# Hybrid decoder trunk: where in the projection's order the state space outputs, the attention weighing and the recurrent gates stand

## The reference, cut to what matters

```python
for l in range(2):
    h = x * (1 + scale) + shift                      # scale, shift, gate from cond @ w_ada[l]
    proj = h @ w_in[l]                               # 2048 -> 6144, twelve chunks of 512
    pa, pb, pc, pd = split(proj)
    y_a = a_b * causal_conv3(a_c * a_x) * silu(a_g)
    y_b = dilated_attention(q, k, v) * silu(b_g)     # 8 heads of 64, three dilation patterns, relative bias
    xc  = causal_conv4(c_x) + bias                   # recurrent branch
    r, i = sigmoid(xc @ wa + ba), sigmoid(xc @ wx + bx)      # 8 blocks of 64 x 64: the gates
    y_c = scan(a(r), sqrt(1 - a*a) * i * xc) * silu(c_g)
    bu  = d_u @ B                                    # complex, 16 channels -> 64 states, 32 groups: the drives
    s   = complex_scan(lambda, bu)
    y_d = glu(gelu(Re(C @ s) + D * d_u)) * silu(d_g) # Re(C @ s): the state space outputs
    x = layer_norm(ALPHA * x + (1 + gate) * (concat(y_a, y_b, y_c, y_d) @ w_out[l]))
```

## Time and profile before

| | |
|---|---|
| median of three runs | 1719.42 us (1717.12 to 1720.55) |
| the profiled execution | 1719.88 us |
| its span | 1718.1 us |
| PE matmul busy | 1653.5 us (96%) |
| DVE busy | 1164.0 us (68%) |
| ACT busy | 754.4 us (44%) |
| POOL busy | 179.4 us (10%) |
| mean granted clock of PE | 0.982 |
| DMA | 373.58 MB, 217 GB/s over the span |

### The profile page before, as it was taken

One profiled execution on the slowest core, in us unless ns is written; L12 is line 12 of the kernel. 1 busy time (PEld: TensorE's weight loads), 2 busy tenths in 40 slices (PEclk: granted clock), 3 DMA queues, 4 the chain that ended last, 5 costly groups with the idle time before them and its releaser, 6 DMA issues.

```text
span 1718.1 us, 22890 instructions
## 1 busy us (share of the span) xinstructions
PE 1653.5 (96%) x7696; PEld 1269.4 (74%) x7696; DVE 1164.0 (68%) x2325; ACT 754.4 (44%) x988; POOL 179.4 (10%) x245
## 2 busy tenths in 40 slices
PE   5889999999999999999999999999999999999996
PEld 0347778778777877878887777777877777777885
DVE  1438975995697589657867685588378458743758
ACT  1316535554553555421127454654555465432112
POOL 2001111111111111000001111111111111100000
PEclk9799999999999999999999999999999999999998
DMA  9998899999999998978748888888988888775524
GB/s 364 339 317 212 204 245 245 219 220 221 242 226 231 238 220 204 215 248 274 246 145 203 196 206 195 205 199 208 209 203 208 192 200 204 188 184 218 196 94 116
DMA packets 317297, 373.58 MB, mean 217 GB/s; under 512 B 30584, under 2 KB 227536, under 8 KB 314512
## 3 DMA queue, kind: packets, MB, share of 16 engines
q1 hardware_dynamic: 288608, 270.57, 49.4%
q0 software_dynamic: 27936, 101.72, 33.1%
q10 hardware_dynamic: 656, 0.17, 0.0%
HBM read 263.89 MB, written 10.99 MB: 160 GB/s over the span
## 4 chain that ended last, share of the span: by engine, by line
PE 74%; DVE 17%; DMA 5%; issue 3%; ACT 1%; DVEq 0%; SPq 0%; ACTq 0%
PE bank L1232 19%; PE bank L1187 15%; PE bank L1197 15%; PE bank L1188 14%; DVE work L1562 6%; DMA pro<-in_w_ada 4%; PE bank L1219 2%; DVE work L1421 1%; DVE work L1422 1%; DVE y_t L1570 1%; PE bank L915 1%; DVE carry L1570 1%; DVE ada_acc L1570 1%; PE bank L1127 1%; PE bank L966 1%
## 5 line engine op out<-in xcount | busy, mean ns | idle before, releaser
L1187 PE MATMUL bank<-op,w_hi 128*128 128x512 f32 x1456 | 581.5, 399 | 0.2 <-ACT w_hi L671 0.2
L1188 PE MATMUL bank<-op,w_hi 128*128 128x512 f32 x1456 | 569.1, 391 | 0.0
L671 ACT ACTIVATE w_hi<-raw 128x1024 fp32r<-128x1024 f32 x188 | 199.2, 1059 | 418.9 <-PE bank L1188 286.5
L1197 PE MATMUL bank<-op,w_lo 128*128 128x512 f32 x1456 | 361.9, 391 | 3.6 <-DMA w_lo<-raw 3.6
L1187 PEld LDWEIGHTS bank<-op,w_hi 128*128 128x128 f32 x1456 | 274.1, 188 | 77.7 <-issue 21.6
L1197 PEld LDWEIGHTS bank<-op,w_lo 128*128 128x128 f32 x1456 | 273.7, 188 | 62.7 <-DMA w_lo<-raw 6.0
L1188 PEld LDWEIGHTS bank<-op,w_hi 128*128 128x128 f32 x1456 | 274.3, 188 | 56.6 <-issue 1.9
L604 POOL DMA_DIRECT2D w_lo<-raw x190 | 165.3, 870 | 1333.3 <-ACT w_lo L674 1124.3
L674 ACT ACTIVATE w_lo<-raw 128x1024 fp32r<-128x1024 f32 x188 | 198.4, 1055 | 98.1 <-PE bank L1197 96.6
L1232 PE MATMUL bank<-w_hi,op 128*128 128x512 f32 x960 | 232.2, 392 | 2.1 <-ACT op L861 2.1
L1232 PEld LDWEIGHTS bank<-w_hi,op 128*128 128x128 f32 x960 | 181.0, 189 | 41.0 <-issue 3.2
(11 more groups left out here) (228 smaller groups left out, 1521.1 us busy)
## 6 DMA issues: line engine op xcount, KB each, us to landing
raw<-in_w_in SPq DMA_DIRECT2D x192, 512.0 KB, 4.6
w_lo<-raw POOLq DMA_DIRECT2D x190, 512.0 KB, 5.3
ada_in<-in_w_ada SPq DMA_DIRECT2D x256, 256.0 KB, 4.6
pro<-in_w_ada SPq DMA_DIRECT2D x32, 1024.0 KB, 10.1
raw<-in_w_out SPq DMA_DIRECT2D x64, 512.0 KB, 4.7
y_t<-in_x SPq DMA_DIRECT2D x2, 2048.0 KB, 12.9
bias_t<-bias_rows_scratch SPq DMA_DIRECT2D x16, 256.0 KB, 5.7
y_t<-in_x SPq DMA_DIRECT2D x4, 1024.0 KB, 8.1
```

The lines of the kernel that those rows point to most:

```text
L671: act.activation(w_hi[:, n % NHL, :], raw[:, n % NRAW, :], ACT.Copy).then_inc(s.hi_done.sem, 1)
L1187: pe.matmul(o, w_hi[:, n % NHL, w], op_hi[k], start=k == 0, stop=False)
L1188: mm = pe.matmul(o, w_hi[:, n % NHL, w], op_lo[k], start=False, stop=False)
L1197: mm = pe.matmul(o, w_lo[:, m % NHL, w], op_hi[k], start=False, stop=k == KT - 1)
```

## The change

Three placements in PE's order are changed, and nothing else. The gates' `put` now stands behind those of the drives, and its gap is 5 in place of 6 (in layer 0's step 0 the gap stays the same, 7). `s5_outputs` goes from gap 19 to gap 20. `weigh` 0 goes from gap 18 to 20 and `p_turn` 1 from 18 to 20; `weigh` 1 goes from 20 to 21 and `p_turn` 2 from 20 to 21; `p_turn` 0 (16) and `weigh` 2 (22) stay. So gap 20 now holds `s5_outputs`, `weigh` 0, `p_turn` 1; gap 21 `weigh` 1, `p_turn` 2; gaps 6, 18 and 19 are empty. The programs of ACT, DVE, SP and POOL are the same as before.

```diff
                     first = l == 0 and begun
                     put(EARLY if first else 3, s5_turn)
-                    put(EARLY + 3 if first else 6, lru_gates)
                     for q, at in enumerate((EARLY + 2 if first else 5, EARLY + 2 if first else 5, 12, 12)):
                         put(at, s5_drive, q)
-                    put(19, s5_outputs)
+                    put(EARLY + 3 if first else 5, lru_gates)
+                    put(20, s5_outputs)
                     for t, at in enumerate((9, 10, 12, 13)):
                         put(at, scores, t)
                     put(10, v_turn)
-                    for g, (at_turn, at_weigh) in enumerate(((16, 18), (18, 20), (20, 22))):
+                    for g, (at_turn, at_weigh) in enumerate(((16, 20), (20, 21), (21, 22))):
                         put(at_weigh, weigh, g)
                         put(at_turn, p_turn, g)
                     put(HALF - 1, ada_sum)
```

## The result

| | before | after |
|---|---|---|
| median | 1719.29 us (1717.12 to 1720.97, 6 runs) | 1754.0 us (1746.8 to 1758.48, 6 runs) |
| profiled execution, its span | 1719.88, 1718.1 us | 1753.59, 1751.8 us |
| mean granted clock | 0.982 | 0.980 |

The ratio is 1.0197, 95% interval 1.0177 to 1.0218: slower by 34 us, where I had forecast slower by 4.

The account below looks back on a forecast made before the run. PE, 96% busy, was taken to bound the kernel, so waits and change-overs removed were set against late low weights: -4.7 - 1.9 + 6.0 + 4.8 = +4.2, a median of about 1723.6 us, 80% range 1713.5 to 1730.

Parts of the forecast that it names:

- Part A: Outputs in layer 0's steps 1 to 3: their wait for DVE goes, 1.56 a time, three times, -4.7 us.
- Part B: Merged outputs, weighing and turning: fewer PE change-overs, 0.24 a step over eight steps, -1.9 us (0 to -3.3).
- Part C, the gates behind the drives: Gap 5 on PE: an exit of 0.13 us saved in each of seven steps.
- Part C, the issue of tile 9's add DMA: ACT's table load begins 0.90 later, so tile 9's add DMA goes out at 311.08 in place of 310.18.
- Part C, its landing: Tile 9's add DMA lands in 6.1 us, costing 0.85 a step, seven times: +6.0.
- upper half of the range: Tile 9's landing cost, range -0.9 to +31 (+1.7 to +12 for 5.5 to 7.0): larger costs likelier by the DMA page.
- Part D: End of a step: tile 22's low weights just due, tile 23's late in seven steps, +4.8 us (0 to +12).
- What would show it: Signs: no outputs' wait; tile 9 waits 0.5 to 1; L1197 DMA waits 15 or more; ACT waits 7 at n = 21.
- The second rival: Tile 9 not late, its add DMA landing in 5.0 or less: about -7, 1712.4 us; chance 0.18.
- the first: Rival: only tile 9 late, add DMAs of tiles 22 and 23 landing within 5.5: +0.4, 1719.8 us; chance 0.32.
- The third, bunching: Rival: landings of 7.0 at tiles 9 and 23, C +12 and D +8, 1733 us; chance 0.05.

Follow-up runs that it names:

- experiment 5: Changed kernel with tile 11's raw load, and the w_ada pieces SP issues behind it, held back by one tile; 1741.22 us in one run.
- experiment 6: Changed kernel with only the w_ada pieces that follow tile 11's raw load issued one tile later; 1758.44 us in one run.
- Experiment 9: Kernel of experiment 1 with SP's small loads and tile 22's second place of w_ada pieces behind raw of tile 23; 1719.48 us, ratio 1.0007.
- experiment 1: Changed kernel with the gates put back in gap 6, the groups in gaps 20 and 21 staying; 1727.7 us, ratio 1.0045.
- experiment 8: Kernel of experiment 1 with ACT's second copy of probabilities, b_g and third copy all behind its split of tile 22; 1728.89 us, ratio 1.0073.
- experiment 4: Changed kernel, but ACT makes tile 10's low weights only after tile 9's add DMA has landed; 1754.41 us in one run.
- filled kernel: Changed kernel with ten more 128x512 matmuls between tile 9's high passes and low pass, except in layer 0's step 0; 1741.4 us in one run.

## Why the prediction was wrong

The direction was right, the size was not: +34 for +4.2. By its own steps:

- **Part A** (-4.7): -4.7 measured, DVE's three waits gone. Right.
- **Part B** (-1.9): -2.1 measured, 0.27 a step for the 0.24 taken. Right.
- **Part C, the gates behind the drives** (-0.13 a step): wrong. 3.03 for 1.29 + 1.76 is 0.02. The Trainium skill (TensorEngine Tiling (Array Packing), Key Properties) has a change of tiling mode drain TensorE, and by it nothing was to be saved here; the trace agrees with that to 0.02 us.
- **Part C, the issue of tile 9's add DMA** (1.03 later, by tile 8's low pass): 1.03 measured. Right.
- **Part C, its landing**: this is the step that failed. "I take 6.1, nearest tile 9's own row" was to give 0.85 a step; it landed in 7.5 and the step cost 2.6, 18.0 in seven for the 6.0. I treated the landing as a property of the transfer, with a little added. It is a property of what goes out beside it: in layer 0's step 1, 4.6 with the load and the pieces held back, 7.0 with the load alone, 7.3 to 7.5 with the w_ada pieces too. Before, the add DMA had a lead of 1.1 us on the load, and landed in 5.8. The delay of 1.03 used that lead up, so it was paid twice: once as delay, once as 1.7 more of landing. The prediction named this load, but gave the case of 7.0 a chance of 0.05. The Trainium skill (DMA: Bandwidth & Descriptors, Queues, rings and completion order) has each DMA engine take turns between its queues packet by packet. Experiments 5 and 6 agree with what the prediction drew from that, a later landing beside a load (4.6 against 7.0); the turns themselves no run here shows. That reading favoured the upper half of the range, and the 18.0 lie above even the +12 that a landing of 7.0 was to give.
- **Part D** (+4.8): +17.1, of which 2.7 at tile 22, 6.3 at tile 23, and 8.1 at tile 0 and the rest, which the sum did not have. The times of issue were right within 0.2 us (c + 5.8 for c + 6.0 at tile 22, `raw` at c + 5.0 for c + 5.1). The 9.0 at tiles 22 and 23 are about twice the sum, again by landings (7.5 for the 6.7 taken from the earlier trace rows): four w_ada pieces and `raw` of tile 23 now stand directly ahead of tile 22's add DMA. Experiment 9 takes `raw` and two of the four pieces away from there and gets 5.0. Layer 0 step 0, at 3.6 for the 1.5 taken, was the worst.
- **Not in the sum at all: the clock.** Some 4.6 us at tile 10 and 5.8 at tile 0 are matmuls at half clock behind stands of PE, a third of the whole loss. A wait was priced at its length, and cost up to 5.8 more.
- **What would show it**: the wait at tile 9 was there in seven steps, but 2.1 to 2.5 long (a cost of 2.2 to 2.7) and not 0.5 to 1; the waits for `w_lo` rose to 29.2 on PE (39.2 on the weight loads); ACT waits up to 7.9 at n = 21. The views named were the right ones.

The second rival, tile 9 not late at all, fell; of the first, tile 23 was on time in six of eight steps, but tile 22's add DMA landed in 6.7 to 8.0, never within the rival's 5.5. The third, bunching, had the mechanism, and at 1733 was still 21 short, half of that by the clock.

One difference has nothing to do with the edits. In the profiles of experiments 1 and 8, tile 11 of layer 0's step 0 cost 1.6 less than before, and tiles 16 and 17 cost 4.9 more; in the other kernels, the kernel after among them, they did not. The traces tell how. In all of them PE stands 2.1 to 2.2 us ahead of tile 11; behind that stand the granted clock falls in the other eleven profiles and does not in these two, which saves them 1.6. So PE comes to tile 15 that much sooner, and `raw` of tile 18, with two loads of biases behind it, goes out at 202.43 in experiment 1, 0.63 ahead of tile 16's add DMA, where it goes out 0.98 behind it in the kernel after. That add DMA lands in 8.0 and not 6.5, and PE stands, and the clock falls:

```profile
211.11 3.78 PE L1197 MATMUL bank<-op,w_lo 128*128 128x512 f32 x8 [3.50 <-DMA w_lo<-raw]
```

So 1.6 us won ahead of a transfer cost 4.9 behind it. Why the clock stayed up in these two stays open, and so does the wait alone, with no change of order about it, against the clock: no run tries it.

## What to carry to other kernels

Before a transfer is moved, look at what is issued near it on the other queues, here from some 3 us ahead of it to 1 us behind: its landing is no property of the transfer. A delay that eats the lead on the next load costs the delay and the longer landing (1.03 and 1.7 here), but a lead is no guarantee: with 2.5 us of it, and two w_ada pieces and an add DMA close ahead, the landing was 7.6 and 7.9. When work of one engine moves, move the in-order engines' reading of it and the loads that wait for it too: as made, the change cost 1754 us, and 1728.54 with ACT's gate block one tile earlier; with the gates in their old gap it was 1727.7 with the old orders of ACT and SP, and 1716.55 with both put right. And price a wait of the tensor engine of 2 us or more at more than its length: in 14 of 28 such places it cost 1.5 to 3.1 us beyond it.

## What the hardware showed that I had not expected

The granted clock fell behind stands of PE as short as 1.95 us (experiment 6, layer 1's step 3; in experiment 4 one of 2.04, then 3.13 for a low pass that takes 1.98), and did not behind others of 2.07 to 2.55 in the kernel after; a step lost about 1.5, 3.1 or 5.8 us by it. What decides between them the runs don't show, only that work in the same place prevents it.

A low pass that had to wait for its `w_lo` takes 0.13 us longer, with no fall of the clock (tile 10's cost in most such steps; the distance from tile 9's start holds tile 9's low pass). It does not need a long stand: in the filled kernel, where PE waited 0.05 to 0.26 us in six of seven steps, it was 0.13 to 0.18 (the low pass at 318.11 takes 2.11 for 1.98), and 0.02 in the step in which it waited for nothing.

A 512 KB add DMA landed in 4.6 us with the loads beside it held back, in 6.7 to 8.0 with a 512 KB load issued within 0.11 us of it, in 8.7 just behind two such loads, and in 7.9 with none within 2.4 us but two w_ada pieces (256 KB each) 1.5 and 0.7 ahead and another add DMA in flight.
